# Two norm stages moved into their neighbours, and fewer zero products, in a two-block transformer kernel

## The reference

```
h_lat = rms_norm(x,   norm_pre_mix[0]) * (1 + sc1)  + sh1
h_ctx = rms_norm(ctx, norm_pre_mix[0]) * (1 + sc1c) + sh1c
y_lat, y_ctx = even_mixer(h_lat, h_ctx, ...)        # grouped-query attention | HGRN2
x   = x   + g1  * rms_norm(y_lat, norm_post_mix[0])
ctx = ctx + g1c * rms_norm(y_ctx, norm_post_mix[0])
h_lat = rms_norm(x,   norm_pre_ffn[0]) * (1 + sc2)  + sh2
h_ctx = rms_norm(ctx, norm_pre_ffn[0]) * (1 + sc2c) + sh2c
x, ctx = x + g2 * rms_norm(conv_ffn(h_lat)), ctx + g2c * rms_norm(conv_ffn(h_ctx))
# layer 1 begins with the same pre-mix norm, then neighbourhood attention with a learned bias
```

## Time and profile before

| what | us |
|---|---|
| median of 3 runs | 2338.86 |
| the 3 runs | 2337.22, 2338.86, 2342.80 |
| time of the profiled execution | 2336.96 |
| its span, first to last instruction | 2335.2 |
| PE busy in the span | 2257.6 |
| mean granted TensorE clock | 0.987 of full speed |

### The profile page before, as it was taken

One profiled execution on the slowest core, in us unless ns is written; L12 is line 12 of the kernel. 1 busy time (PEld: TensorE's weight loads), 2 busy tenths in 40 slices (PEclk: granted clock), 3 DMA queues, 4 the chain that ended last, 5 costly groups with the idle time before them and its releaser, 6 DMA issues. The chain is left out here.

```text
span 2335.2 us, 37624 instructions
## 1 busy us (share of the span) xinstructions
PE 2257.6 (97%) x14328; PEld 1837.8 (79%) x14328; DVE 1432.8 (61%) x2345; ACT 1148.1 (49%) x1978; POOL 80.0 (3%) x117
## 2 busy tenths in 40 slices
PE   9999999999999999999999997999999989999998
PEld 7887887888888877887568886688888777877887
DVE  6665367567665457666567666475555544447887
ACT  3444465444443464444477666343433444547555
POOL 0000000000000000000002222000000000000000
PEclk9999999999999999999999999999999979999999
DMA  8886427875887435883121110243433443305663
GB/s 263 271 258 214 93 99 234 260 252 162 261 257 239 116 119 165 261 264 112 37 72 46 47 65 20 73 126 119 125 108 99 145 108 91 100 1 168 193 189 108
DMA packets 390082, 346.76 MB, mean 148 GB/s; under 512 B 24404, under 2 KB 353352, under 8 KB 389448
## 3 DMA queue, kind: packets, MB, share of 16 engines
q1 hardware_dynamic: 380173, 294.55, 42.5%
q10 hardware_dynamic: 9787, 50.52, 5.5%
HBM read 343.99 MB, written 1.05 MB: 148 GB/s over the span
## 5 line engine op out<-in xcount | busy, mean ns | idle before, releaser
L813 PE MATMUL ps<-x_hi_lo,gu_hi 128*128 128x512 f32 x1680 | 423.9, 394 | 1.6 <-DVE gu_sum L1013 1.6
L813 PEld LDWEIGHTS ps<-x_hi_lo,gu_hi 128*128 128x128 f32 x1680 | 305.6, 188 | 80.8 <-issue 17.5
L1013 DVE TENSOR_REDUCE gu_sum<-ps 128x256 f32<-128x512 f32 x220 | 150.6, 689 | 240.4 <-PE ps L815 240.0
L910 ACT ACTIVATE gu_hi<-w_gu 128x1024 fp32r<-128x1024 f32 x218 | 227.4, 1055 | 120.2 <-DVE gu_sum L1013 49.0
L996 DVE TENSOR_TENSOR gu_lo<-w_gu,gu_hi 128x1024 fp32r<-128x1024 f32 x218 | 258.9, 1219 | 18.6 <-ACT gu_hi L910 18.4
L815 PEld LDWEIGHTS ps<-x_hi_lo,gu_lo 128*128 128x128 f32 x1680 | 228.8, 190 | 16.8
L815 PE MATMUL ps<-x_hi_lo,gu_lo 128*128 128x256 f32 x1680 | 233.7, 282 | 0.0
L842 PE MATMUL ps<-dn_hi,h_hi 128*128 128x512 f32 x440 | 173.5, 394 | 5.3 <-DVE h_lo L1042 5.2
L842 PE MATMUL ps<-dn_lo,h_hi 128*128 128x512 f32 x440 | 172.4, 392 | 0.0
L842 PE MATMUL ps<-dn_hi,h_lo 128*128 128x512 f32 x440 | 171.3, 389 | 0.0
L927 ACT ACTIVATE silu<-gu_sum 128x256 f32<-128x256 f32 x88 | 36.8, 418 | 257.2 <-DVE gu_sum L1013 256.5
(11 more groups left out here) (552 smaller groups left out, 4738.7 us busy)
## 6 DMA issues: line engine op xcount, KB each, us to landing
w_gu<-in_ffn_w_up SPq DMA_DIRECT2D x176, 512.0 KB, 6.3
w_dn<-in_ffn_w_down SPq DMA_DIRECT2D x132, 512.0 KB, 3.5
w_mod<-in_w_mod ACTq DMA_DIRECT2D x64, 768.0 KB, 7.5
w_gu<-in_ffn_w_gate SPq DMA_DIRECT2D x88, 512.0 KB, 5.1
odd_w<-in_odd_w_qkv SPq DMA_DIRECT2D x24, 512.0 KB, 5.2
w_gu<-in_ffn_w_down SPq DMA_DIRECT2D x11, 1024.0 KB, 4.9
hgrn_w<-in_even_w_in SPq DMA_DIRECT2D x20, 512.0 KB, 4.0
wo<-in_w_out SPq DMA_DIRECT2D x2, 4096.0 KB, 13.2
```

What stands on the lines that cost most here:

```text
L813: pe.matmul(gu(a), gu_hi[n][:, a, f, :], x_both[:, f, :, :], start=(f == 0), stop=False, skip_group_check=True)
L910: act.activation(gu_hi[n][:, a, :, :], wgu[n][:, a, :, :], ACT.Copy).then_inc(s["w_hi"], 1)
L1013: dve.reduce_sum(c[n][:, a, :], gu(a).rearrange("p h t -> p t h"), AX.X).then_inc(s["c_ready"], 1)
```

## The change

Three edits. (1) The first pre-norm and `gqa_project` become one stage. A new class `FirstNorm` has the norm's instructions; DVE multiplies x, the modulation and the inverse root in one operation per tile and stream, the context stream first, ACT then adds the shift, and PE projects the token tiles in the order 2, 3, 0, 1 as soon as the context's eight tiles are there. Six zero products stand behind the sums in place of eleven. SP issues the projection's loads and the HGRN weights in one list. (2) The squares, sums, root, reciprocal and spreading of the two-stream norm ahead of the FFN go to the end of `out_both_phase`: `post_add` signals each added tile, ACT squares all 16 pieces of 256 columns, PE sums each piece for itself (32 f32 products of one column in place of 16), ACT, DVE and PE finish with root, reciprocal and spreading. `ffn_both_phase` begins with `scaled`; its seven zero products become four; ACT mixes the weight rounding into the roundings of x, and `first_gate_up` takes n as its outer loop. (3) The pre-norm with the bias ends with one zero product in place of four.

```
-    ALONE, ADDED, OWN = (0, 1, 2), (3, 4), (5, 6, 7)      # class Norm: both engines squared
+    def squares(self, act, s, st):
+        for f in range(FT):
+            act.wait_ge(s["x_added"], st * FT + f + 1)
+            act.activation(self.part(self.sq, f, st), self.part(self.k.x_T, f, st), ACT.Square).then_inc(s["sq_done"], 1)
...
+    def sums(self, pe, s):
+        for st in range(2):
+            for f in range(FT):
+                pe.wait_ge(s["sq_done"], st * FT + f + 1)
+                for tt in range(TT):
+                    last = pe.matmul(self.k.ps[:, 4, st * TT + tt:st * TT + tt + 1], self.part(self.sq, f, st)[:, tt * P:(tt + 1) * P], self.k.ones[:, 0:1],
+                                     start=(st == 0 and f == 0 and tt == 0), stop=(f == FT - 1), skip_group_check=True)
+        last.then_inc(s["sum_done"], 1)
...
                 def first_gate_up():
-                    for f in range(FT):
-                        pe.wait_ge(s["x_hi"], f + 1)
-                        for n in range(2):
+                    for n in range(2):
+                        for f in range(FT):
+                            if n == 0:
+                                pe.wait_ge(s["x_hi"], f + 1)
                             for a in range(2):
...
-                idle_products(pe, k, 2, 3)
-                norm.sums(pe, s)
-                norm.spread(pe, s)
-                idle_products(pe, k, 3, 4)
+                idle_products(pe, k, 2, 4)
...
-                norm.squares(act, s)
-                norm.root(act, s)
-                for n in range(2):
-                    hi_gu(n, n, 0, n)
-                    hi_gu(n, n, 1, n)
-                norm.rounded(act, s, x_hi)
+                for f in range(FT):
+                    norm.rounded(act, s, f, x_hi)
+                    if f in (2, 4):
+                        hi_gu(0, 0, f // 2 - 1, 0)
+                hi_gu(1, 1, 0, 1)
+                hi_gu(1, 1, 1, 1)
...
-                idle_products(pe, k, 7, 4 if bias else 11)
+                idle_products(pe, k, 7, 1 if bias else 11)
...
+class FirstNorm:
+    STREAMS = (1, 0)
+    def sums(self, pe, s):
+        ...
+        pe.matmul(k.ps[:, 0, :], k.ones[:, :], self.total, start=False, stop=True).then_inc(s["sum_done"], 1)
+        idle_products(pe, k, 7, 6)
...
+        for i, st in enumerate(self.STREAMS):
+            for f in range(FT):
+                act.wait_ge(s["n_done"], i * FT + f + 1)
+                h = b.h_T[:, f, st * S:(st + 1) * S]
+                act.activation(h, h, ACT.Identity, bias=b.mod[:, 0, f, st:st + 1]).then_inc(s["h_done"], 1)
...
+        for st in self.STREAMS:
+            for f in range(FT):
+                at = slice(st * S, (st + 1) * S)
+                dve.scalar_tensor_tensor(b.h_T[:, f, at], k.x_T[:, f, at], b.mod[:, 0, FT + f, st:st + 1], self.r[:, at], ALU.mult,
+                                         ALU.mult).then_inc(s["n_done"], 1)
...
+    ORDER = (2, 3, 0, 1)                                   # gqa_project
...
+                for dst, src in first_ahead:
+                    sp.dma_start(dst, src).then_inc(s["first_in"], 16)
                 load_ahead(sp, s, ahead)
...
+                norm.sums(pe, s)
+                pe.wait_ge(s["first_in"], 16 * len(first_ahead))
+                for i, tt in enumerate(ORDER):
+                    if i % TT == 0:
+                        pe.wait_ge(s["h_done"], FT * (i // TT + 1))
...
                 turn_tensor(pe, k, s, t[1].z, s["po_turned"], 1, 0)     # out_both_phase
+                norm.sums(pe, s)
+                norm.spread(pe, s)
...
                     post_scalar(act, k, s, t[st], st)
+                for st in range(2):
+                    norm.squares(act, s, st)
+                norm.root(act, s)
...
-                prenorm_phase(nc, k, b, 0, [0, 1], gqa_ahead, first=True)
-                gqa_project(nc, k, b, m, hgrn, hgrn_weights)
+                gqa_project(nc, k, b, m, hgrn, gqa_ahead, hgrn_weights)
```

More of the change, by code:

```diff
@@ L358, in post_scale, with post_add, post_vector @@
             dve.tensor_scalar(t.z[:, tt, BANK:D], k.ps[:, at + 1, :], t.rstd[:, tt:tt + 1], None, ALU.mult).then_inc(s["z1_ready"], 1)
-def post_add(dve, k, s, gain, cols, st=0, bank=4):
+def post_add(dve, k, s, gain, cols, st=0, bank=4, added=None):
     for f in range(FT):
         dve.wait_ge(s["po_turned"], st * (FT // 2) + f // 2 + 1)
-        dve.scalar_tensor_tensor(k.x_T[:, f, cols:cols + S], turned(k, f, bank), gain(f), k.x_T[:, f, cols:cols + S],
-                                 ALU.mult, ALU.add)
-def post_vector(dve, k, s, t, gain, cols, st=0, bank=4):
+        last = dve.scalar_tensor_tensor(k.x_T[:, f, cols:cols + S], turned(k, f, bank), gain(f), k.x_T[:, f, cols:cols + S],
+                                        ALU.mult, ALU.add)
+        if added:
+            last.then_inc(added, 1)
+def post_vector(dve, k, s, t, gain, cols, st=0, bank=4, added=None):
     post_scale(dve, k, s, t, st)
-    post_add(dve, k, s, gain, cols, st, bank)
+    post_add(dve, k, s, gain, cols, st, bank, added)
 def first_tiles(nc, ctx):
@@ L492, in shift, with part @@
         return self.b.mod[:, self.l, 3 * FT + f, st:st + 1]
[L494 to L499, removed]
+    def part(self, a, f, st):
+        return a[:, f, st * S:(st + 1) * S]
+    def squares(self, act, s, st):
+        for f in range(FT):
+            act.wait_ge(s["x_added"], st * FT + f + 1)
+            act.activation(self.part(self.sq, f, st), self.part(self.k.x_T, f, st), ACT.Square).then_inc(s["sq_done"], 1)
@@ L513, in sums @@
-    def sums(self, pe, s):
[L514 to L522, removed]
+        act.activation(self.std, self.k.ps[:, 4, 0:2 * TT], ACT.Sqrt, bias=self.k.eps[:, 1:2], scale=1.0 / D).then_inc(s["std_done"], 1)
@@ new lines, in inverse @@
+    def inverse(self, dve, s):
+        dve.wait_ge(s["std_done"], 1)
+        dve.reciprocal(self.r, self.std).then_inc(s["r_done"], 1)
+    def sums(self, pe, s):
+        for st in range(2):
[4 more added lines that the diff above has]
+                                     start=(st == 0 and f == 0 and tt == 0), stop=(f == FT - 1), skip_group_check=True)
@@ L527, in spread @@
         pe.wait_ge(s["r_done"], 1)
[L528 to L546, removed]
+        for tt in range(2 * TT):
+            pe.matmul(self.k.ps[:, 1, tt * P:(tt + 1) * P], self.r[:, tt:tt + 1].broadcast_to([P, P]), self.k.ident[:, :], start=True, stop=True,
+                      skip_group_check=True)
@@ L557, in scaled, with rounded @@
             last.then_inc(s["n_done"], 1)
+    def rounded(self, act, s, f, x_hi):
+        act.wait_ge(s["n_done"], f + 1)
+        for st in range(2):
+            last = act.activation(self.part(x_hi, f, st), self.part(self.b.h_T, f, st), ACT.Identity, bias=self.shift(f, st))
+        last.then_inc(s["x_hi"], 1)
     def rest(self, dve, s, f, x_hi, x_lo):
         dve.wait_ge(s["x_hi"], f + 1)
-        for i, st in enumerate(self.streams):
-            last = dve.scalar_tensor_tensor(self.part(x_lo, f, i), self.part(self.b.h_T, f, i), self.shift(f, st), self.part(x_hi, f, i).bitcast(F32),
+        for st in range(2):
+            last = dve.scalar_tensor_tensor(self.part(x_lo, f, st), self.part(self.b.h_T, f, st), self.shift(f, st), self.part(x_hi, f, st).bitcast(F32),
@@ L2408, in gqa_project @@
+def gqa_project(nc, k, b, m, hgrn, first_ahead, ahead):
+    names = ["ahead_in", "h_hi", "h_lo", "w_hi", "w_lo", "k0_done", "p_done", "p_used", "copied", "qk_sq_done", "ss_done", "std_done", "step", "rot_done", "turned"]
     NQK = GQ + GKV
@@ L2410, in gqa_project @@
     WEIGHTS_AT = (1, 2)
+    ORDER = (2, 3, 0, 1)
+    norm = FirstNorm(nc, k, b)
+    names += FirstNorm.names
     with ExitStack() as ctx:
@@ L2417, in gqa_project @@
         kd = sb("k_twice", [P, 2 * TT, GKV, 2, HD2])
+        norm.allocate(ctx)
         with phase(nc, names) as (block, s):
@@ L2473, in _ @@
             def _(dve):
+                norm.vector(dve, s)
                 c = Chain(dve, s["step"])
                 half = HD2 // 2
[L2476 removed]
+                dve.wait_ge(s["first_in"], 16 * len(first_ahead))
+                for i, tt in enumerate(ORDER):
                     qk = m.qk[:, tt, :].rearrange("p (h d) -> p h d", d=HD2)
[L2478 removed]
+                    dve.wait_ge(s["qk_sq_done"], i + 1)
                     dve.reduce_sum(ss[:, :], sq[:, :].rearrange("p (h d) -> p h d", d=HD2), AX.X).then_inc(s["ss_done"], 1)
[L2480 removed]
+                    dve.wait_ge(s["std_done"], i + 1)
                     c.link(dve.reciprocal(r[:, :], std[:, :]))
@@ L3725, in out_both_phase @@
         t = [ln_buffers(nc, ctx) for st in range(2)]
+        std, r = (ctx.enter_context(nc.sbuf_tensor(f"both_{x}", [P, 2 * TT], F32)) for x in ("std", "r"))
+        norm = Norm(k, b, l, b.y_T, std[:, :], r[:, :])
         def gain(st):
@@ L3781, in _ @@
                 for st in range(2):
```

(3 more changed lines are left out.)

113 lines of the change are left out of this document (67 added, 46 removed).

## The result

The changed kernel takes 2347.12 us (median of 7, 2344.05 to 2352.06) against 2338.86 before: a ratio of 1.0033, 95% interval 1.0023 to 1.0044, or +8.3 us (+5.4 to +10.3). The forecast was 2341.9, range 2333.5 to 2348.5. The time lies inside the range, and on the line between "within 0.3%" (0.75) and "slower" (0.16), a little beyond it. The direction was right, but the +3.0 was too small, and the time lies 1.1 above 2335 to 2346, the range that the prediction gave for its forecast alone.

The account below looks back on a forecast made before the run. The prediction took PE, busy for 97% of the span, to bound the kernel. Edits 1 to 3 summed as -1.0 + 6.0 - 2.0 = +3.0 on the median 2338.86, giving 2341.9 us, range 2333.5 to 2348.5.

Parts of the forecast that it names:

- the bounds' ends added: Over all three edits, the extremes of their bounds summed: from -4.7 to +7.9 us.
- the slower rival: Third joint: clock stays at 0.50 through three groups of 32 products; +4.6 there, total +9.6, 2348.5 us; chance 0.11.
- the clock term: End of projection: key and query transposes slowed by a fallen clock behind PE's gap; 0.8 us, bounds 0 and 3.2.
- The start: First joint: PE starts the projection at about 1115.8 in place of 1120.33, -4.5 us.
- over 3 us of room: Projection's start: HGRN loads could push back the last small loads, with over 3 us to spare.
- The exposed rotary step: End of projection: the last tile, now latent, has six more operations that nothing covers; +2.65 us.
- The clock was forecast to fall at 1502: Second joint: the clock falls to half during the moved sums, at 1502; early end 1500.3, other end not at all.
- The sums' end: Output stage's tail: 64 passes, 22 before the clock falls and 42 after, end at 1511.2; bounds 1507.1 and 1512.7.
- the stage started: FFN stage: starts at 1514.2 after root, reciprocal and spreading, about 1 us after the old scaling; bounds 1509.0 and 1515.7.
- The first round: FFN's first products: end 17.5 us after the stage's start, where they ended 12.5 after the scaling began before.
- the last rounded weight half: FFN's first round: PE can't use this half until 13.8 us after the stage's start, then has 15 products at 0.245.
- The rival built on it: Second joint: the sums hold the clock at full, edit 2 costs +0.8, total -2.2, 2336.7 us; chance 0.12.

Follow-up runs that it names:

- e1: The kernel before with only the first norm and projection made one stage, context first; ratio 1.0002, +0.5 us.
- e4: e1 with tiles in the order context, latent, latent, context and HGRN loads issued only after the first loads land; 0.9988 against the kernel before, -2.8 us.
- e2: The kernel before with only the two-stream norm's sums moved into the output stage's tail; ratio 1.0031, +7.3 us.
- e5: e2 with the latent stream's squares and additions done under the context stream's matmuls, 36 passes of sums instead of 64; 0.9994 against the kernel before, -1.4 us.
- e6: e2 with the first two gate and up tiles loaded and rounded in the output stage, products f outside; 1.0011 against the kernel before, +2.6 us.
- e7: All three edits on the kernel before, with the tile order and later loads of e4, short sums of e5, early weights of e6; 0.9954, -10.8 us.
- e9: e7 with one zero product in place of four at the FFN stage's start; 0.9950 against the kernel before, -11.7 us.
- e3: The kernel before with only one zero product in place of four behind the bias products; ratio 0.9995, -1.2 us.
- e8_order_only: e1 with the tile order context, latent, latent, context alone, HGRN loads right behind the first loads; one profiled execution, no measured ratio.

## Why the prediction held, and where it was too small

That the time lies inside the stated range is in part luck. It lies above the forecast's own 2346, and by 0.3 even above the bounds' ends added, 2338.86 + 7.9 = 2346.8. What the range holds beyond that was given for the slower rival, a clock that doesn't come back at the third joint, and there it came back.

All three joints by the same two events in each execution, in us:

| joint, from - to | before | after | edit alone | mended |
|---|---|---|---|---|
| 1: root ready - first scores | 59.18 | 60.21 | 58.67 (e1) | 54.75 (e4) |
| 2: last transposes - end of first round | 27.41 | 33.16 | 34.86 (e2) | 28.68 (e5), 27.12 (e6), 22.61 (e7), 20.08 (e9) |
| 3: end of bias products - third group of 32 | 16.25 | 15.03 | 15.47 (e3) | |

**Edit 1: the mechanism was right, and the clock term was mis-sized.** The start gained 4.1 where 4.5 was forecast; most of the missing part lies in the loads issued right behind, for which the prediction claimed over 3 us of room where there were 2.4. The exposed rotary step cost 2.40 in the wait, forecast 2.65. The step that failed is the 0.8 taken for the transposes behind the gap: they cost 1.4 and 2.65, inside the bounds of 0 to 3.2 but in their middle and upper half. I took the low end because PE had been nearly idle for 3.3 us at the second joint with the clock still at 1.00; that row shows the clock during an idle stretch, not behind it. In the kernel before, too, it stood at 0.50 from 1503.1 on, right behind that very stretch:

```profile
1503.10:1506.40 3.30, 3.30 (x5) 1.35 (x4) 3.20 (x5) 1.93 (x4) 0.00 (x0) 0.50 0.90 251
```

With 2.65 in place of 0.8 the term comes to about +1, which the joint shows.

**Edit 2: right in mechanism, and near in size because two misses nearly cancel.** The clock was forecast to fall at 1502 in the old frame; with the 6.89 by which the transposes were later, it fell at 1508.9 - 6.89 = 1502.0. The sums' end was forecast at 1511.2 and came at 1510.4; the stage started at 1513.3 against 1514.2. The first round then took 18.2 from the stage's start, forecast 17.5. That last step came about in another way: the prediction had PE wait for the last rounded weight half, but PE waits for nothing within its last 31 products; it is late because the clock stood at 0.50 under the first of them, which the sum didn't have. So the stage's start came 0.9 early and the round took 0.7 longer. In e2_sums the clock stood at 0.50 longer under the round (10.10 for the 31 products, 8.86 in the kernel after), and the joint lost 7.45. Net +5.75 in the trace, +7.3 (4.9 to 9.6) alone, forecast +6.0. The rule of the Trainium skill ("TensorE: Matmul & The Clock Gate", section "Why this matters for your kernels") that the clock stays up if TensorE is kept busy without long idle gaps did not hold here: PE was busy for 8.38 of 8.40 us of the sums at 0.50. The rival built on it gave +0.8 and is refuted by e2_sums.

**Edit 3: right, and some 0.8 too favourable.** One zero product saved 3.27 in place of 3.6, and L2890 lost 2.04 in place of 1.6, because the clock came back 5 us into it and not 4. Net -1.2, forecast -2.0, bounds -3.6 to -0.9. The slower rival falls: L2895 and L2901 ran at full clock.

So the sum of the terms as they turned out is about +1.0 + 5.75 - 1.2 = +5.6 in one pair of executions, and +6.6 by the three edits alone, where the forecast had +3.0. The rest up to +8.3 isn't at these joints. Executions of one kernel differ by 6 to 14 us here, as the clock falls in some places in one execution and not in another, and the intervals of the three edits are wide enough to hold the rest. Beside the later runs the kernel before had medians of 2339.95 to 2341.09, 1.1 to 2.2 above the 2338.86 used here, which is about the size of it. Whether any of the rest is due to the change stays open.

## What to carry to other kernels

When a tile with a longer chain is moved to the end of a stage, look for what hides that chain; here the order of four tiles was worth 3.7 us (54.93 in e8_order_only against 58.67 in e1_norm), and the gap cost once as a wait and once more in the products behind it. When sums move ahead of a stage's start, all that the stage used to load and round during them moves onto its path: take the loads along, or leave the sums. And put under the matmuls whatever part of the sums is ready early: 36 passes in place of 64 were worth 6.2 of the 7.45 us that the joint had lost, and by the medians the whole loss of the edit.

## What the runs showed that I had not expected

The first products of a stage need not wait until zero products have lifted the clock: in e9_one_zero_ffn 32 real products took 8.69 with the clock at 0.50 when they began, 0.8 more than behind the four zero products of e7_all_mended, which had put them off by 3.4 more (5.28 from the first zero product to the first real one, 1.86 with one). And a load of 32 KB with two of 512 KB issued right behind it landed 11.5 to 11.9 us after its issue, 9.0 to 9.2 without them.
